# The second MLP matrix by Strassen's seven products, with split weights cached in DRAM

## Chip, cores, metric

One core of a Trainium2 chip. The metric is the device time of the whole program in microseconds (us), from the first to the last instruction of the core; lower is better.

## The reference, cut

```python
# SEQ = 2048 and DEC_SEQ = 512 rows of D_MODEL = 1024; D_FF = 4096; one layer, f32
h = rms_norm(x, norm_mix_g)
x = x + pool_mixer(h, pool_w, pool_scale)      # four channel groups: mean over 2, 4, 8, 16
                                               # neighbouring rows minus the row, then 256x256
h = rms_norm(x, norm_mlp_g)
a = relu(einsum('bsd,df->bsf', h, w_up))       # first matrix, 1024 x 4096
x = x + einsum('bsf,fd->bsd', a * a, w_down)   # second matrix, 4096 x 1024
y = rms_norm(x, final_norm_g)
```

Both inputs (2048 and 512 rows) go through the same layer. The time is nearly all in the two matrices.

## The kernel before

The 2560 rows are five **groups** of 512 rows (GT). A group keeps its normalized, transposed rows `h2` in SBUF and runs over the 4096 hidden columns in 16 **chunks** of 256 (two tiles of 128, FT). All five groups read all weights again.

**Precision by splitting.** Each f32 operand is split in two parts, hi (rounded to the type fp32r) and lo (the rest), and a product is three matmuls: hi x hi, hi x lo, lo x hi. ACT makes hi (a copy that casts), DVE makes lo (a subtraction). This is done to each tile of `w_up` (`wu_raw` to `wu_hi`, `wu_lo`, 128 x 1024), to each chunk of `w_down` (`wd_raw` to `wd_hi`, `wd_lo`) and to the squared activations `a`.

**PE's order** is written out by hand: `up(n+1)`, the first matrix of the next chunk (2 tiles x 8 x 3 matmuls of 512 columns), then `down(n)`, the second matrix (8 outputs x 2 tiles x 3 matmuls), so that activation and splits of a chunk lie behind the other matmuls. `up` writes `up_ps` (2 banks of PSUM), `down` a ring of four banks, `ring_ps`. DVE evicts each bank and adds it to `acc` (`add_down`); PE waits for `ring_read` before it writes a bank again.

**The next group's mixer** is woven into the first eight chunks of a group: for each of four windows ACT normalizes a column block of the rows, PE transposes it (`turn_window`, `turn_halos`), POOL adds neighbours (`window_sums`, window w has w+1 additions of some 1024 elements), DVE and ACT split, PE multiplies (`pool_out`), DVE adds. At a group's end PE also transposes the next group's rows (`transpose`), ACT and DVE make `h2_hi` and `h2_lo` from them, and the finished group is normalized and stored. POOL also squares the activations for `a_lo` (`squares`).

**SP's queue** issues all DMAs, in an order written out by hand, each behind a wait for the buffer to come free: for every chunk two `wu` tiles of 512 KB into two raw buffers, and one 1 MB `wd` chunk. An engine works its queue strictly in order, so a wait holds up all that stands behind it.

**Start and end.** The first group's mixer is done with banded matrices on PE; the last group's final norm and stores follow the last matmul.

Of the kernel before, what the change touches and what calls it, by code (L numbers as in the profile page):

```python
# [6 lines left out]
P = 128  # L27
# [44 lines left out]
FIRST = 0  # L72

SUM_STEPS = [sum(v + 2 for v in range(w)) for w in range(WINDOWS + 1)]


def build(nc, x, halos, w_up, w_down, pool_w, pool_scale, g_mix, g_mlp, g_fin, ends, bands, ident_in,
          out):
# [3 lines left out]
    ds = bass.ds  # L82
# [4 lines left out]
    with ctx:  # L87
# [23 lines left out]
        wd_hi = sb("wd_hi", [P, FT, D], f32r)  # L111
        wd_lo = sb("wd_lo", [P, FT, D], f32r)
        wu_raw = sb("wu_raw", [P, FT, DT, P])
        wu_hi = sb("wu_hi", [P, FT, DT, P], f32r)
        wu_lo = sb("wu_lo", [P, FT, DT, P], f32r)
        wd_raw = sb("wd_raw", [P, FT, D])

        relu = sb("relu", [P, FT, GT])
        square = sb("square", [P, FT, GT])
        a_hi = sb("a_hi", [P, 2, FT, GT], f32r)  # L120
        a_lo = sb("a_lo", [P, 2, FT, GT], f32r)

        wd_last_hi = h2_hi[:, 0:FT * NH, :]
        wd_last_lo = h2_lo[:, 0:FT * NH, :]
        acc = sb("acc", [P, TT, D])
# [5 lines left out]
        sums = [sb(f"sums{i}", [P, CT, HT]) for i in range(2)]  # L131
        end_scale = sb("end_scale", [P, WINDOWS, CT, 2, HALO])
        dt_hi = sb("dt_hi", [P, CT, GT], f32r)
        dt_lo = sb("dt_lo", [P, CT, GT], f32r)
        junk = dt_hi[:, :, :].rearrange("p c t -> p (c t)")
        x1 = sb("x1", [P, TT, D])
        pw_hi = sb("pw_hi", [P, WINDOWS * CT, WC], f32r)
        pw_lo = sb("pw_lo", [P, WINDOWS * CT, WC], f32r)
        g_fin_b = sb("g_fin_b", [P, D])
# [15 lines left out]
        ms_end = sb("ms_end", [P, 1])  # L155
        me_end = sb("me_end", [P, 1])
# [3 lines left out]
        pw_raw = acc[:, 0:2, :].rearrange("p a (b e) -> p (a b) e", e=WC)  # L160
        scale_b = acc[:, 2, :]


        row_squares = [x1[:, i, :] for i in range(TT)] + [junk]
        first_squares = square[:, :, :].rearrange("p c t -> p (c t)")

        wd_room = [wd_lo[:, t, :].rearrange("p (c t) -> p c t", c=CT) for t in range(FT)]
        first_dt = [(dt_hi[:, :, :], dt_lo[:, :, :]), wd_room,
                    (a_hi[:, 0, :, :], a_hi[:, 1, :, :]), (a_lo[:, 0, :, :], a_lo[:, 1, :, :])]
# [18 lines left out]
        acc_moved = sem("acc_moved")  # L188
# [19 lines left out]
        ring_read = sem("ring_read")  # L208
        xr_in = [sem(f"xr_in{j}") for j in range(TT)]
# [8 lines left out]
        pw_in = [sem(f"pw_in{w}") for w in range(WINDOWS)]  # L218
        banded = sem("banded")
# [28 lines left out]


        def ring_base(g):  # L250
            return FIRST_OUTS + g * GROUP_OUTS

        LAST_BASE = ring_base(GROUPS - 1)
        MIX_END = MIX_PAIRS * MIX_PAIR_OUTS

        def window_sums(engine, eng, w, ht, room, done_sem, done):

# [16 lines left out]

        @block.sync
        def _(sp):
            def load_wu(k, t):

                sp.dma_start(wu_raw[:, t, :, :], w_up[k, t]).then_inc(wu_in[t], 16)

            def next_wu(n, k):
                for t in range(FT):
                    sp.wait_ge(wu_lo_done, FT * (n - 1) + t + 1)
                    load_wu(k, t)

            def load_wd(k):
                sp.dma_start(wd_raw[:, :, :], w_down[k]).then_inc(wd_in, 16)

            def step(n, k, k_next):
                next_wu(n + 1, k_next)
                sp.wait_ge(wd_lo_done, FT * n)
                load_wd(k)
# [4 lines left out]

            def load_halos(m):  # L300
                sp.dma_start(xh[:, :], halos[m]).then_inc(halo_in, 16)

            def load_ends(m):
                sp.dma_start(end_scale[:, :, :, :, :], ends[m]).then_inc(ends_in, 16)

            def store(g):
                for j in range(TT if g is not LAST else TT - 1):
                    sp.wait_ge(final_done, TT * g + j + 1)
                    sp.dma_start(out[g, j * P:(j + 1) * P, :], acc[:, j, :]).then_inc(acc_moved, 16)
                if g is LAST:  # L310

                    j = TT - 1
                    for h in range(NH):
                        c = slice(h * HALF, (h + 1) * HALF)
                        sp.wait_ge(final_done, TT * g + j + 1 + h)
                        sp.dma_start(out[g, j * P:(j + 1) * P, c], acc[:, j, c]).then_inc(acc_moved, 16)

            def prefetch_rows(m):
                sp.wait_ge(transposed, DT * m)
                load_rows(m)  # L320
                sp.wait_ge(xw_done, NORMS * WINDOWS * (m - 1))
                load_halos(m)
                sp.wait_ge(summed, SUM_STEPS[WINDOWS] * (m - 1))
                load_ends(m)
# [9 lines left out]
            sp.dma_start(scale_b, pool_scale.partition_broadcast(P)).then_inc(acc_moved, 16)  # L334
# [5 lines left out]
            sp.dma_start(g_fin_b[:, :], g_fin.partition_broadcast(P)).then_inc(gain_in, 16)  # L340
            for t in range(FT):
                load_wu(0, t)
            load_wd(0)
            load_ends(1)
            load_halos(1)
            next_wu(1, 1)
            sp.wait_ge(transposed, DT)
            load_rows(1)
            next_wu(2, 2)

            def group(g, mixer, prefetch):
                n0 = CHUNKS * g
                sp.wait_ge(wd_lo_done, 2 * (n0 + 1))
                load_wd(1)
                with sp.Fori(2, CHUNKS - 1) as k:
                    step(n0 + k, k, k + 1)
                if mixer:
# [5 lines left out]
                if prefetch:  # L363
                    prefetch_rows(g + 2)
                if mixer:
                    next_wu(n0 + CHUNKS + 2, 2)
# [811 lines left out]
```

## Time and profile before

| | |
|---|---|
| runs | 1880.66, 1882.22, 1882.68 us; median 1882.22 |
| profiled execution | span 1879.7 us; the profile gives no other time of its own, so the span stands for it; the median of the runs is 2.5 us above |
| PE, DVE, ACT, POOL busy | 99%, 59%, 37%, 18% |
| granted TensorE clock | 0.997 of 2.4 GHz on average |
| DMA | 194.84 MB, 104 GB/s over the span, queue q1 29.7% of the 16 engines' time |

A page's group row reads: line, engine, operation, written tile <- read tiles, shape, count | busy us, mean ns of one | idle time of the engine just before, and who ended it. Matmuls overlap, so the mean of one (390 ns) is longer than the distance between two.

### The profile page before, as it was taken

What the parts mean: (1) busy time and instruction counts of PE and PEld (TensorE: products, weight loads), DVE (VectorE), ACT (ScalarE), POOL (GpSimd) and SP (SyncE); (2) the same over time, 40 slices, a digit from 0 to 9 for tenths busy, and PEclk for the clock granted to TensorE, in tenths of its full rate; (3) what the DMA queues carried; (4) which work ended last, traced back from release to release, by engine and by line L of the source; (5) the groups of instructions that cost most, each with busy time, mean ns of one, the idle gap of its engine ahead of it and who ended that gap; (6) DMA issues with size and microseconds to landing.
All of it is one profiled execution on the core that took longest, in us unless ns stands there. A gap on an engine that the chain in (4) does not pass through costs nothing.

```text
span 1879.7 us, 24832 instructions
## 1 busy us (share of the span) xinstructions
PE 1858.7 (99%) x8598; PEld 1548.4 (82%) x8598; DVE 1108.7 (59%) x1323; ACT 702.0 (37%) x1012; POOL 330.8 (18%) x300
## 2 busy tenths in 40 slices
PE   8999999999999999999999999999999999999998
PEld 7888888888888888888888888888888888888887
DVE  5566655566666555666665556566745575555555
ACT  5533342245333422453334224433352342233232
POOL 3222310012223100112231011222310110001011
PEclk9999999999999999999999999999999999999999
DMA  6422222243222222422222324322232232223221
GB/s 212 159 88 89 80 100 100 90 146 127 90 89 89 90 89 89 170 102 90 89 89 89 101 100 160 110 84 84 82 110 99 91 135 101 89 89 104 99 88 67
DMA packets 43975, 194.84 MB, mean 104 GB/s; under 512 B 5132, under 2 KB 7052, under 8 KB 33684
## 3 DMA queue, kind: packets, MB, share of 16 engines
q1 hardware_dynamic: 43924, 194.34, 29.7%
q14 instruction: 41, 0.34, 0.1%
q8 instruction: 10, 0.16, 0.0%
HBM read 183.84 MB, written 10.49 MB: 103 GB/s over the span
## 4 chain that ended last, share of the span: by engine, by line
PE 94%; DVE 3%; issue 2%; ACT 1%; DMA 0%; POOL 0%; SPq 0%; DVEq 0%; ACTq 0%; POOLq 0%
PE ring_ps L937 15%; PE ring_ps L939 15%; PE ring_ps L938 15%; PE up_ps L918 14%; PE up_ps L916 14%; PE up_ps L917 14%; DVE a_lo L621 1%; PE ring_ps L976 1%; PE ring_ps L978 1%; PE ring_ps L977 1%; PE mix_ps L997 1%; DVE wd_lo L615 1%; PE mix_ps L959 1%; DMA first_x<-x 0%; ACT wd_hi L389 0%
## 5 line engine op out<-in xcount | busy, mean ns | idle before, releaser
L629 DVE TENSOR_TENSOR acc<-ring_ps,acc 128x512 f32<-128x512 f32 x600 | 412.6, 690 | 420.6 <-PE ring_ps L939 419.3
L937 PE MATMUL ring_ps<-wd_hi,a_hi 128*128 128x512 f32 x1264 | 496.8, 393 | 5.2 <-DVE a_lo L621 2.7
L916 PE MATMUL up_ps<-h_hi,wu_hi 128*128 128x512 f32 x1280 | 499.9, 391 | 0.0
L917 PE MATMUL up_ps<-h_lo,wu_hi 128*128 128x512 f32 x1280 | 498.3, 389 | 0.0
L918 PE MATMUL up_ps<-h_hi,wu_lo 128*128 128x512 f32 x1280 | 498.2, 389 | 0.0
L939 PE MATMUL ring_ps<-wd_hi,a_lo 128*128 128x512 f32 x1264 | 492.5, 390 | 0.0
L938 PE MATMUL ring_ps<-wd_lo,a_hi 128*128 128x512 f32 x1264 | 492.0, 389 | 0.0
L821 POOL TENSOR_TENSOR square<-relu 128x512 f32<-128x512 f32 x160 | 176.5, 1104 | 1241.2 <-ACT relu L396 1198.3
L609 DVE TENSOR_TENSOR wu_lo<-wu_raw,wu_hi 128x1024 fp32r<-128x1024 f32 x158 | 202.6, 1282 | 219.0 <-ACT wu_hi L383 219.0
L389 ACT CAST wd_hi<-wd_raw 128x1024 fp32r<-128x1024 f32 x158 | 158.2, 1051 | 413.9 <-PE ring_ps L939 296.7
L937 PEld LDWEIGHTS ring_ps<-wd_hi,a_hi 128*128 128x128 f32 x1264 | 237.4, 188 | 56.8 <-DVE acc L629 5.0
L396 ACT ACTIVATE relu<-up_ps 128x512 f32<-128x512 f32 x160 | 95.6, 598 | 500.0 <-PE up_ps L918 500.0
L918 PEld LDWEIGHTS up_ps<-h_hi,wu_lo 128*128 128x128 f32 x1280 | 240.3, 188 | 50.0
L917 PEld LDWEIGHTS up_ps<-h_lo,wu_hi 128*128 128x128 f32 x1280 | 240.4, 188 | 49.0
L916 PEld LDWEIGHTS up_ps<-h_hi,wu_hi 128*128 128x128 f32 x1280 | 240.4, 188 | 48.9 <-DVE h_lo L654 0.2
L939 PEld LDWEIGHTS ring_ps<-wd_hi,a_lo 128*128 128x128 f32 x1264 | 237.2, 188 | 49.5
L938 PEld LDWEIGHTS ring_ps<-wd_lo,a_hi 128*128 128x128 f32 x1264 | 237.5, 188 | 47.8
L615 DVE TENSOR_TENSOR wd_lo<-wd_raw,wd_hi 128x1024 fp32r<-128x1024 f32 x158 | 220.9, 1439 | 51.6 <-ACT wd_hi L389 51.6
L383 ACT CAST wu_hi<-wu_raw 128x1024 fp32r<-128x1024 f32 x160 | 165.8, 1036 | 0.0
L621 DVE TENSOR_TENSOR a_lo<-square,a_hi 128x512 fp32r<-128x512 f32 x160 | 125.9, 827 | 0.0
L398 ACT ACTIVATE a_hi<-relu 128x512 fp32r<-128x512 f32 x160 | 101.2, 633 | 5.1
L267 POOL TENSOR_TENSOR sums<-sums 128x1024 f32<-128x1024 f32 (+3 forms) x24 | 66.4, 2766 | 1.9
(134 smaller groups left out, 854.2 us busy)
## 6 DMA issues: line engine op xcount, KB each, us to landing
wu_raw<-w_up SPq DMA_DIRECT2D x160, 512.0 KB, 3.3
wd_raw<-w_down SPq DMA_DIRECT2D x80, 1024.0 KB, 4.8
xr<-x SPq DMA_DIRECT2D x20, 512.0 KB, 7.0
out<-acc SPq DMA_DIRECT2D x19, 512.0 KB, 2.9
first_x<-x SPq DMA_DIRECT2D x4, 512.0 KB, 8.6
acc<-pool_w SPq DMA_DIRECT2D x4, 256.0 KB, 10.4
acc<-pool_scale SPq DMA_DIRECT2D x1, 512.0 KB, 10.3
g_fin_b<-g_fin SPq DMA_DIRECT2D x1, 512.0 KB, 10.7
```

The costliest lines, as they stand in the source:

```text
L383: nc.scalar.copy(wu_hi[:, t, :, :], wu_raw[:, t, :, :]).then_inc(wu_hi_done, 1)
L389: nc.scalar.copy(wd_hi[:, t, :], wd_raw[:, t, :]).then_inc(wd_hi_done, 1)
L609: nc.vector.tensor_tensor(wu_lo[:, t, :, :], wu_raw[:, t, :, :], wu_hi[:, t, :, :].bitcast(f32), ALU.subtract).then_inc(wu_lo_done, 1)
L615: nc.vector.tensor_tensor(wd_lo[:, t, :], wd_raw[:, t, :], wd_hi[:, t, :].bitcast(f32), ALU.subtract).then_inc(wd_lo_done, 1)
L629: nc.vector.tensor_tensor(acc[:, j, c], ring_ps[:, o % RING, :], base[:, j, c], ALU.add).then_inc(ring_read, 1)
L821: nc.gpsimd.tensor_tensor(square[:, t, :], relu[:, t, :], relu[:, t, :], ALU.mult).then_inc(square_done, 1)
L916: nc.tensor.matmul(o, wu_hi[:, t, d, :], h2_hi[:, d, :], start=(d == 0), stop=False)
L917: nc.tensor.matmul(o, wu_hi[:, t, d, :], h2_lo[:, d, :], start=False, stop=False)
L918: last = nc.tensor.matmul(o, wu_lo[:, t, d, :], h2_hi[:, d, :], start=False, stop=(d == DT - 1))
L937: nc.tensor.matmul(dst, a_hi[:, slot, t, r], hi, start=(t == 0), stop=False)
L938: nc.tensor.matmul(dst, a_hi[:, slot, t, r], lo, start=False, stop=False)
L939: last = nc.tensor.matmul(dst, a_lo[:, slot, t, r], hi, start=False, stop=(t == FT - 1))
```

## The change

The second matrix is computed by Strassen's algorithm in Winograd's form. A **step** n is 512 hidden columns of a group (8 steps a group, STEPS = 40). It has four tiles u = 4n to 4n+3 of the first matrix. Its share of the second matrix, activations (512 rows x 512 hidden) times weights (512 hidden x 1024, taken as two column halves), is cut into 2 x 2 quadrants, and seven products of quadrant sums take the place of eight. Product q = 7n+k writes two banks at once; the order is P5, P6, P1, P3, P4, P7, P2. Each product is summed over the 8 steps of a group in one of seven f32 accumulators (`m_acc`), and the seven are combined once per group (`combine_first`, `combine_rest`), after which `finish` scales the rows.

- PE: per step 12 matmuls a product, 84 instead of 96; the first matrix, the mixer and all column counts are unchanged. The products run one step behind the tiles: `step(n)` interleaves tiles 4n to 4n+3 with products q0 to q0+6, q0 = 7(n-1).
- DVE: sums of activation quadrants (`sum_a`, four of 512 elements a step) and, in group 0 only, of weight quadrants (`sum_w`, four of 1024); seven a splits of 512; seven evictions of 1024 (before: sixteen of 512).
- Weights of the second matrix: in group 0 the raw quadrants are loaded (two 1 MB loads a step), summed, split into one of three `w_slot`s, used, and stored to a DRAM cache (56 stores of 1 MB). In groups 1 to 4 SP loads the split operands back from the cache, seven 1 MB loads a step; `wd` is no more split there.
- `wu_raw` has one buffer instead of two.
- The square is now ACT's (`activate` squares in place), POOL has no squares. hi of a is an ACT copy.
- The pooling weights' split is cached in DRAM too and loaded for each window. The windows are woven into steps 3 to 6 of a group, its statistics into steps 2 and 7.
- Everything is unrolled; there are no loops in the program.

Core of the diff (in the order of the file; the parts left out are of the same pattern):

```diff
+P5, P6, P1, P3, P4, P7, P2 = range(7)
+NP = 7
+A_SLOTS = 2
+W_SLOTS = 3
+CACHED = PAIRS * NP
...
+            def load_wu(u):
+                if u > 0:
+                    sp.wait_ge(wu_lo_done, u)
+                s, f = u // FP % PAIRS, u % FP
+                sp.dma_start(wu_raw[:, :, :], w_up[2 * s + f // FT, f % FT]).then_inc(wu_in, 16)
+            def load_raw(n, k):
+                if n > 0:
+                    sp.wait_ge(w_lo_done, NP * (n - 1) + (P7 if k == 0 else P2) + 1)
+                sp.dma_start(wd_raw[:, 2 * k:2 * k + 2, :], w_down[2 * n + k]).then_inc(raw_in[k], 16)
+            def move_w(q):
+                if q < CACHED:
+                    sp.wait_ge(w_lo_done, q + 1)
+                    sp.dma_start(w_cache[q], slot).then_inc(w_stored[i], 16)
+                elif q < PRODUCTS:
+                    sp.wait_ge(ring_full, TURN[q - W_SLOTS] + 1)
+                    if q - W_SLOTS < CACHED:
+                        sp.wait_ge(w_stored[i], 16 * stores_of_slot(q))
+                    sp.dma_start(slot, w_cache[q % CACHED]).then_inc(w_in[i], 16)
...
+            def step(n):
+                q0 = NP * (n - 1)
+                if n > 0:
+                    move_w(q0 + 3)
+                load_wu(4 * n + 3)
+                if n > 0:
+                    move_w(q0 + 4)
+                    move_w(q0 + 5)
+                if 0 < n < PAIRS:
+                    load_raw(n, 0)
+                load_wu(4 * n + 4)
+                if n > 0:
+                    move_w(q0 + 6)
+                if 0 < n < PAIRS:
+                    load_raw(n, 1)
+                move_w(q0 + 7)
+                load_wu(4 * n + 5)
+                move_w(q0 + 8)
+                move_w(q0 + 9)
+                load_wu(4 * n + 6)
+            for n in range(STEPS + 1):
+                step(n)
+                if is_boundary(n):
+                    store(n // PAIRS - 1)
...
+            def split_wu(u):
+                act.wait_ge(wu_in, 16 * (u + 1))
+                if u >= FT:
+                    act.wait_ge(up_done, u - FT + 1)
+                nc.scalar.copy(wu_hi[:, u % FT, :, :], wu_raw[:, :, :]).then_inc(wu_hi_done, 1)
...
+            def boundary(n):
+                for k in range(3):
+                    split_h2(g, 2 * k)
+                    split_h2(g, 2 * k + 1)
+                    split_a(q0 + 2 + k)
+                    split_w(q0 + 3 + k)
+                split_h2(g, DT - 2)
+                split_h2(g, DT - 1)
+                split_a(q0 + 5)
+                split_w(q0 + 6)
+                activate(4 * n)
+                split_wu(4 * n + 2)
+                split_a(q0 + 6)
+                activate(4 * n + 1)
+                split_wu(4 * n + 3)
+                final_stats(g - 1)
...
+            def step(n):
+                split_wu(4 * n + 2)
+                if n > 0:
+                    evict(q0 + 0)
+                    split_a(q0 + 2)
+                    evict(q0 + 1)
+                    split_w(q0 + 3)
+                    split_a(q0 + 3)
+                    sum_a(n - 1, P7)
+                    split_w(q0 + 4)
+                split_wu(4 * n + 3)
+                if n > 0:
+                    evict(q0 + 2)
+                    split_a(q0 + 4)
+                    split_w(q0 + 5)
+                    evict(q0 + 3)
+                    split_a(q0 + 5)
+                    split_w(q0 + 6)
+                if windows:
+                    subtract_own(g + 1, w)
+                    split_pooled(g + 1, w)
+                split_wu(4 * n + 4)
+                if n > 0:
+                    evict(q0 + 4)
+                    split_a(q0 + 6)
+                sum_w(n, P5)
+                sum_w(n, P7)
+                split_w(q0 + 7)
+                sum_w(n, P6)
+                if n > 0:
+                    evict(q0 + 5)
+                split_w(q0 + 8)
+                sum_w(n, P4)
+                if windows:
+                    add_pooled(g + 1, w)
+                split_wu(4 * n + 5)
+                sum_a(n, P5)
+                split_a(q0 + 7)
+                sum_a(n, P6)
+                if n > 0:
+                    evict(q0 + 6)
+                split_a(q0 + 8)
+                sum_a(n, P3)
+                split_w(q0 + 9)
...
+            def product(q):
+                r, a, b = TURN[q], q % A_SLOTS, q % W_SLOTS
+                pe.wait_ge(a_lo_done, q + 1)
+                if q < CACHED:
+                    pe.wait_ge(w_lo_done, q + 1)
+                else:
+                    pe.wait_ge(w_in[b], 16 * loads_of_slot(q))
+                if r >= 2:
+                    pe.wait_ge(ring_read, r - 1)
...
+            def step(n):
+                up_tile(4 * n)
+                if windows:
+                    turn_window(g + 1, w)
+                product(q0 + 0)
+                product(q0 + 1)
+                if windows:
+                    turn_halos(g + 1, w)
+                up_tile(4 * n + 1)
+                product(q0 + 2)
+                product(q0 + 3)
+                up_tile(4 * n + 2)
+                product(q0 + 4)
+                product(q0 + 5)
+                if windows:
+                    pool_out(g + 1, w)
+                up_tile(4 * n + 3)
+                product(q0 + 6)
+            def boundary(n):
+                pe.wait_ge(x1n_done, TT * g)
+                for k in range(4):
+                    transpose(g, 2 * k)
+                    transpose(g, 2 * k + 1)
+                    product(q0 + k)
+                pe.wait_ge(h2_lo_done, DT * (g + 1))
+                up_tile(4 * n)
+                product(q0 + 4)
+                product(q0 + 5)
+                up_tile(4 * n + 1)
+                product(q0 + 6)
+                up_tile(4 * n + 2)
+                up_tile(4 * n + 3)
```

`boundary(n)` stands in place of `step(n)` at n = 8, 16, 24, 32, the first step of a group. DVE's boundary has, between the split pairs of `h2`, one eviction, a split (and w split in group 0's last products) each; then `combine_first` (five additions of 1024), `split_wu(4n+2)`, evictions 4 and 5 with split 6, `combine_rest` (two), `split_wu(4n+3)`, eviction 6, `split_wu(4n+4)`, `finish`, `split_wu(4n+5)` and the first sums and splits of step n.

## Rows read from the trace of the kernel before

**Rows 1.** The page's busy times: engine, us, share of the span, instructions.

```profile
PE 1858.7 (99%) x8598; PEld 1548.4 (82%) x8598; DVE 1108.7 (59%) x1323; ACT 702.0 (37%) x1012; POOL 330.8 (18%) x300
```

**Rows 2.** Waits of PE, the longest of its MLP's: us in total, times, longest.

```profile
PE ring_ps L937 <- DVE a_lo L621: 2.7, 4, 0.7
```

**Rows 3.** Timeline of PE: first, two middle and last 512-column matmul; start, length.

```profile
42.67 0.50 PE L916 MATMUL up_ps<-h_hi,wu_hi 128*128 128x512 f32 x1
...
499.77 0.39 PE L918 MATMUL up_ps<-h_hi,wu_lo 128*128 128x512 f32 x1
...
516.99 0.39 PE L937 MATMUL ring_ps<-wd_hi,a_hi 128*128 128x512 f32 x1
...
1872.76 0.39 PE L939 MATMUL ring_ps<-h_hi,a_lo 128*128 128x512 f32 x1
```

**Rows 4.** Timeline of PE: the first and last of 20 pooling matmuls; eight transposes.

```profile
28.39 0.28 PE L976 MATMUL ring_ps<-pw_hi,wd_lo 128*128 128x256 f32 x1
...
30.64 0.28 PE L977 MATMUL ring_ps<-pw_lo,wd_lo 128*128 128x256 f32 x1
...
387.76 1.03 PE L997 MATMUL mix_ps<-ident,xr 128*128 128x128 f32 x8
```

**Rows 5.** Timeline of DVE, splits with nothing on POOL.

```profile
57.48 1.23 DVE L609 TENSOR_TENSOR wu_lo<-wu_raw,wu_hi 128x1024 fp32r<-128x1024 f32 x1 [4.14 <-ACT wu_hi L383]
58.62 2.35 DVE L615 TENSOR_TENSOR wd_lo<-wd_raw,wd_hi 128x1024 fp32r<-128x1024 f32 x2
60.90 1.29 DVE L621 TENSOR_TENSOR a_lo<-square,a_hi 128x512 fp32r<-128x512 f32 x2
```

**Rows 6.** The page's groups: an eviction, and ACT's two sizes.

```profile
L629 DVE TENSOR_TENSOR acc<-ring_ps,acc 128x512 f32<-128x512 f32 x600 | 412.6, 690 | 420.6 <-PE ring_ps L939 419.3
...
L383 ACT CAST wu_hi<-wu_raw 128x1024 fp32r<-128x1024 f32 x160 | 165.8, 1036 | 0.0
...
L398 ACT ACTIVATE a_hi<-relu 128x512 fp32r<-128x512 f32 x160 | 101.2, 633 | 5.1
```

**Rows 7.** The page's DMA issues: KB each, median us from issue to landing.

```profile
wu_raw<-w_up SPq DMA_DIRECT2D x160, 512.0 KB, 3.3
wd_raw<-w_down SPq DMA_DIRECT2D x80, 1024.0 KB, 4.8
...
out<-acc SPq DMA_DIRECT2D x19, 512.0 KB, 2.9
```

**Rows 8.** Timeline of SP's queue at a group boundary: start, length, issue.

```profile
406.04 0.33 SPq L289 DMA_DIRECT2D wd_raw<-w_down  x1
406.64 2.09 SPq L298 DMA_DIRECT2D xr<-x  x4
...
411.51 0.34 SPq L281 DMA_DIRECT2D wu_raw<-w_up  x1
```

**Rows 9.** Line L298 (xr), its last three issues of 406.64 to 408.73.

```profile
DMA to landing us min/median/max: 6.7/7.4/8.5
```

**Rows 10.** DMA issues: the wu load of 411.51 alone.

```profile
wu_raw<-w_up SPq DMA_DIRECT2D x1, 512.0 KB, 6.9
```

**Rows 11.** Timeline of DVE and POOL in window 3: work side by side.

```profile
223.13 8.46 POOL L267 TENSOR_TENSOR sums<-sums 128x1048 f32<-128x1048 f32 x3
...
222.01 4.99 DVE L615 TENSOR_TENSOR wd_lo<-wd_raw,wd_hi 128x1024 fp32r<-128x1024 f32 x2 [0.70 <-ACT wd_hi L389]
```

**Rows 12.** Windows of the start: busy of PE PEld DVE ACT POOL, PEclk, DMA.

```profile
9.00:12.00 3.00, 0.34 (x4) 0.16 (x2) 0.34 (x1) 1.15 (x2) 0.75 (x2) 1.00 1.03 249
12.00:15.00 3.00, 2.83 (x14) 2.83 (x15) 1.66 (x4) 1.15 (x2) 1.23 (x2) 0.56 1.04 380
```

**Rows 13.** Timelines of the end: ACT, DVE, SP; start, length.

```profile
1873.91 0.63 ACT L408 ACTIVATE dt_hi<-acc 128x512 fp32r<-128x512 f32 x1 [0.20 <-DVE acc L629]
...
1873.18 0.69 DVE L629 TENSOR_TENSOR acc<-ring_ps,acc 128x512 f32<-128x512 f32 x1 [0.24 <-PE ring_ps L939]
...
1876.56 0.99 SPq L316 DMA_DIRECT2D out<-acc  x2
```

More of the change, by code:

```diff
@@ L278, in _ @@
         def _(sp):
[L279 to L294, printed above, removed]
+            def load_wu(u):
+                if u >= UPS:
+                    return
+                if u > 0:
[7 more added lines that the diff above has]
+            def move_w(q):
+                i = q % W_SLOTS
+                slot = w_slot[:, i, :, :, :].rearrange("p s k e -> p (s k e)").bitcast(f32)
+                if q < CACHED:
[6 more added lines that the diff above has]
+                    sp.dma_start(slot, w_cache[q % CACHED]).then_inc(w_in[i], 16)
             def load_rows(m):
@@ L339, in _ @@
             sp.dma_start(g_mlp_c[:, :], g_mlp).then_inc(gain_in, 16)
[L340 to L357, printed above, removed]
-                    step(n0 + CHUNKS - 1, CHUNKS - 1, 0)
-                    step(n0 + CHUNKS, 0, 1)
-                else:
-                    sp.wait_ge(wd_lo_done, 2 * (n0 + CHUNKS - 1))
-                    load_wd(CHUNKS - 1)
[L363 to L366, printed above, removed]
-                store(g)
@@ L376, in _ @@
+            for n in range(STEPS + 1):
+                step(n)
+                if is_boundary(n):
+                    store(n // PAIRS - 1)
+            sp.wait_ge(out_moved, 16 * TT * GROUPS)
         @block.scalar
         def _(act):
-            def split_wu(n, t, first=False):
-                act.wait_ge(wu_in[t], 16 * (n + 1))
-                if not first:
-                    act.wait_ge(up_done, FT * (n - 1) + t + 1)
-                nc.scalar.copy(wu_hi[:, t, :, :], wu_raw[:, t, :, :]).then_inc(wu_hi_done, 1)
@@ L605, in _ @@
+            for n in range(STEPS):
+                if is_boundary(n):
+                    boundary(n)
+                else:
+                    step(n)
+            for k in range(2, NP):
+                split_a(NP * (STEPS - 1) + k)
+            final_stats(LAST)
         @block.vector
         def _(dve):
-            def split_wu(n, t):
-                dve.wait_ge(wu_hi_done, FT * n + t + 1)
-                nc.vector.tensor_tensor(wu_lo[:, t, :, :], wu_raw[:, t, :, :], wu_hi[:, t, :, :].bitcast(f32),
-                                        ALU.subtract).then_inc(wu_lo_done, 1)
@@ new lines, in _ @@
+            for n in range(STEPS):
+                if is_boundary(n):
+                    boundary(n)
+                else:
+                    step(n)
+            q0 = NP * (STEPS - 1)
+            evict(q0 + 0)
+            split_a(q0 + 2)
+            evict(q0 + 1)
+            split_a(q0 + 3)
+            sum_a(STEPS - 1, P7)
+            evict(q0 + 2)
+            split_a(q0 + 4)
+            evict(q0 + 3)
+            split_a(q0 + 5)
+            combine_first(LAST)
+            evict(q0 + 4)
@@ L813, in _ @@
+            split_a(q0 + 6)
+            evict(q0 + 5)
+            combine_rest(LAST)
+            evict(q0 + 6)
+            finish(LAST)
         @block.gpsimd
         def _(pool):
-            def squares(n, first=False):
-                for t in range(FT):
-                    pool.wait_ge(relu_done, FT * n + t + 1)
-                    if not first:
-                        pool.wait_ge(a_lo_done, FT * (n - 1) + t + 1)
-                    nc.gpsimd.tensor_tensor(square[:, t, :], relu[:, t, :], relu[:, t, :],
-                                            ALU.mult).then_inc(square_done, 1)
@@ L1024, in _ @@
                 pe.wait_ge(pool_lo, w + 1)
+                part = slice(w * CT, (w + 1) * CT)
                 for j in range(TT):
@@ L1091, in _ @@
[L1091 to L1103 removed]
+            for f in range(FP):
+                up_tile(f, next_tile if f == 0 else lambda d: None)
@@ L1106, in end_scales @@
+            for n in range(1, STEPS):
+                if is_boundary(n):
+                    boundary(n)
+                else:
+                    step(n)
+            for k in range(NP):
+                product(NP * (STEPS - 1) + k)
 def end_scales():
```

886 lines of the change are left out of this document (474 added, 412 removed).

## Prediction

> **What bounds the kernel now.** I read the page's busy times first: PE is busy for 99% of the span, DVE for 59%, ACT and POOL less [rows 1]. Then the waits: those of the MLP's matmuls are small: the greatest, for `a_lo`, sums to 2.7 us [rows 2]. Then the timeline of PE: the 512-column matmuls follow each other every (516.99-499.77)/76 = 0.2267 us [rows 3], at the full granted clock. So the kernel is TensorE work laid end to end, from the first matmul of the first matrix at 42.67 to the last end at 1873.15, 1830.5 us [rows 3]. The work in it: 7680 matmuls x 0.2267 = 1741.1; 384 of the pooling at 0.118 = 45.5 and about 300 transposes at 0.11 = 33 [rows 4]; some 1820 in all, so PE's own stalls there are about 10.7 us. 42.7 us lie before and 6.6 behind.
>
> **What the change takes away.** Each step of 512 hidden columns costs 84 instead of 96 matmuls for the second matrix, over 40 steps: 480 x 0.2267 = -108.8 us. This is sure as far as PE sets the time. A step is now four tiles of the first matrix at 24 x 0.2267 = 5.44 and seven products at 12 x 0.2267 = 2.72: 40.8 us.
>
> **What must keep up, and its prices.** DVE: a 1024-element subtraction costs 1.22 us alone and 1.14 in a row, 512 elements 0.61 in a row [rows 5]; an eviction of 512 from PSUM is 0.69 [rows 6], so one of 1024 is an estimated 1.14 (0.69 plus another 512 elements, less the overlap). ACT: 1.04 and 0.63 [rows 6]. Handing over to another engine: 0.07 (taken a little above the 0.04 between the end of DVE's last eviction, 1873.87, and ACT's start on it, 1873.91, [rows 13]). DMA: 512 KB land after 3.3 us and 1 MB after 4.8 [rows 7], so 1.8 fixed and 1.5 per 512 KB. Transfers that are issued together queue: behind a 1 MB load issued at 406.04 (by the median landed at 410.9), four of 512 KB landed until 408.4+8.5 = 416.9 (the last was issued at 408.4), 1.5 us each, and a wu load issued at 411.5 behind them took 6.9 instead of 3.3 [rows 8 to 10].
>
> **Groups 1 to 4, ordinary steps: nothing.** DVE per step: four wu splits, seven evictions, seven a splits, four a sums: 4x1.14 + 7x1.14 + 11x0.61 = 19.3 of 40.8. The weights now come by DMA: 7 MB of slots and 2 MB of wu per step, 9x3.0 = 27 of 40.8 us. I walked the SP queue: each slot's load is issued at the end of the product three before; the shortest lead is 10.9 us against 4.8 to 7.8. The single-buffered wu_raw is refilled after its split and has 5 us to spare. So PE sets these steps.
>
> **Group 0: a ring through SP's queue, +139.** Here each product's weights are summed and split on the chip and stored: 7 w splits and 4 w sums more, DVE 19.3+12.5 = 31.9 of 40.8. Throughput is enough; latency isn't. SP's queue alternates `move_w(q)` (waits for the w split of q, then a 1 MB store) and `load_wu(u)`, and DVE's queue puts the split of tile u between the w splits. So each wu load sits behind the store just issued: 1.8+3x1.5 = 6.3 us (1 MB and 512 KB). Walk one round from the end of w split 5 (offset of the product in q0; T=0):
> - store 5, raw load 0 and wu load 4n+4 are queued: 0.1+1.8+5x1.5 = 9.4; ACT hi and DVE lo 2.4: 11.8. Evict 4, a 6, sum P5 are 2.9; sum P7 waits for raw load 1, which ends 9x1.5 of traffic, at 15.4; it and w split 7: 17.8.
> - store 7, wu load 4n+5: 6.4, hi and lo 2.4: 26.5. a sum, a split 7 (hi, lo in turn 1.4), sum, evict 6, a 8, sum, w 9: 6.2: 32.7.
> - store 9, wu load 4n+6 and its splits 8.7: 41.4. Evict 0, a 2, evict 1, w 3: 4.1: 45.5.
> - store 3, wu load 4n+7 and its splits 8.8: 54.3. Evict 2, a 4, w 5: 2.9: 57.2.
>
> The round closes at 57.2 us and PE isn't in it; PE waits at products 6, 0, 2 and 4. In the four steps with a pooling window the third tile also waits for `pool_out`, whose second half needs the eviction of product 5 (late in DVE's queue, at 20): +4.0, and POOL's additions double the time of DVE's SBUF work beside them (two 1024-element splits 4.99 us instead of 2.35, [rows 5, 11]): +1.5. What is queued behind DVE's wu split are evictions and a splits, and PE's next product waits for these.
>
> Start: tiles 0 to 3 run undisturbed to 66.1. From the split of tile 4 at 64.9 sum P5, sum P7 and w split 0 end at 68.3; store 0 and wu load 5 bring that split to 77.1; sums, a splits 0 and 1 and w split 2 follow, to 82.9; store 2 and wu load 6, splits and evictions: w split 3 at 95.7; store 3, wu load 7 and the rest: w split 5 of step 1 at 107.4. Six rounds and four windows: 107.4+6x57.2+4x5.5 = 472.6; 32.7 more, and the boundary of step 8, walked likewise (transposed tiles' splits now in DVE's queue between evictions), ends at 551. Pure PE work would be there at 42.7+36x5.44+56x2.72+15.8 (windows)+5.1 (transposes, first tile) = 411.8. The term is +139. The store behind which a load queues is not in this trace: I take it to cost what a load ahead costs (a store alone takes 2.9 against a load's 3.3 [rows 7], so it moves its bytes about as fast). The bound below is that stores delay no load.
>
> The Trainium skill says the same, in "DMA: Bandwidth & Descriptors", section "Queues, rings and completion order": a completion increment lands only after every earlier write of that DMA engine. The rows show it for loads, none shows it for a store ahead. By it the term stays +139; by independent stores it would be the 58 of the second rival.
>
> **Boundaries 16, 24 and 32: +25.3 each, +76.** PE's order is transposes and products 0 to 3, tile 4n, products 4, 5, tile 4n+1, product 6. SP's is load of slot 3, `load_wu(4n+3)`, slots 4, 5, `load_wu(4n+4)`, slot 6. `load_wu(4n+3)` waits for the split of tile 4n+2, which ACT starts when tile 4n is done: activation 1.2, hi 1.1, lo 1.2 (DVE is still at `combine_first`, 5x1.14), then SP, then 512 KB and 1 MB: 1.8+4.5. So product 4 waits 10.1 us behind tile 4n; product 6 waits for `load_wu(4n+4)` in the same way, 9.9. Ahead of these, product 0 has no tile before it to cover the last sum and split of a (1.9), and the transposes wait for bank reads that stand in DVE's queue between evictions and splits (2.5): 4.4. Product 0 of the next step waits 0.9 for `finish`. The bounds: if SP had slots 4 to 6 issued before the wu loads, 5.4 each; if they queued behind more traffic than these, a few us more.
>
> **Clock: +8.** PE was busy for 0.34 of the three microseconds to 12.0, and in the next three the granted clock was 0.56 (mostly the lower of 1.2 and 2.4 GHz), which loses 0.44x3 = 1.3 [rows 12]. Six pauses of 10 us at the boundaries: 8. In group 0 PE isn't on the path and a slower matmul is hidden.
>
> **End: +8.** In the last seven products `combine_first` stands in DVE before eviction 4 and split 6: 9.3 us from the end of product 3 to product 6 instead of 5.4, and 0.8 at product 0: +4.7. Behind the last matmul, where DVE's last eviction now ends 0.7 us after it: an eviction that ends 1.9 after it, two squares of full rows one after the other (2x1.25, by ACT's 0.63 for half a row and its read-out), then the same root, scale and store as now; 9.9 instead of 6.6: +3.3. The prices are those of the last rows' chain [rows 13].
>
> **Sum**, against the profiled execution's 1879.7: -108.8 -10.7 +139 +76 +8 +8 = 1991; the runs' median is 2.5 above that span: 1994, said as 1995.
>
> **Rivals.**
> - *Faster: the loads are in time.* If the wu load is never what DVE waits for, a step of group 0 is PE-bound (31.9 of DVE in 40.8), and the slots of a boundary arrive before tile 4n ends. Boundaries then cost 5.4 each, 4x5.4 = 22: 1879.7+2.5-108.8-10.7+8+22 = 1793. It decides if a load is on hand about 4 us after w split in all four places; for it speaks that DMA is only 30% busy now (the table above) and that a wu load alone lands in 3.3; against it SP's order, since `load_wu` can't be issued before the store ahead of it, and the lead left by 40.8 us is less than the walk's parts.
> - *Stores don't delay loads.* Only loads queue behind loads. The four parts of the round are then 14.4, 12.4, 10.2 and 9.1: 46.1 us. Seven rounds save 78 and the start 3, so group 0 costs 58 instead of 139; the boundaries, where only loads queue, stay: 1994-81 = 1913.
> - *More in group 0*: halved clock at PE's pauses there reaches the path in the window steps, small stalls in the windows of groups 1 to 3, and a round of 60: 7x2.8 + 4x3 + 8 = 40 more: 2035.
>
> **How the numbers follow.** Forecast 0.56, stores independent 0.16, loads in time 0.14, more in group 0 0.14. The forecast's own range is 1950 to 2020. I take 1885 to 2045, which leaves out the loads in time and part of the last. Within 0.2% (3.8 us, what a measurement of this kernel can tell from no change) and below come only from the first rival and the gap between it and the second: faster 0.14, same 0.02, slower 0.84.
>
> **What would show it.** 3360 matmuls of the second matrix at 0.2267 apart; in group 0 a period of about 57 us with DVE's wu split waiting for ACT, ACT for wu_raw's DMA; PE busy only some 72% there and 99% in ordinary steps later; two pauses of 10 us at each of three boundaries, ended by the slot's DMA, with a lower clock behind them. I am wrong if the period in group 0 is near 41, or if the slots' loads at a boundary land before tile 4n ends.

## The result, and the profile after

The changed kernel takes 2006.7 us (median of four runs, 2003.3 to 2010.8) where the kernel before takes 1881.4 on the same chip: ratio 1.0666, interval 1.0649 to 1.0683. It is 6.7% slower with 480 fewer matmuls. The forecast was 1995, and slower. The profiled execution has a span of 2007.2 us.

The page of the changed kernel: busy times, granted clock in 40 slices, the chain by engine, two groups and the DMA issues.

```profile
PE 1809.7 (90%) x8118; PEld 1493.7 (74%) x8118; DVE 1136.6 (57%) x1178; ACT 762.8 (38%) x1186; POOL 147.1 (7%) x139
...
PE   8878778777999999977999999699999977999996
...
PEclk8998799889999999988999999799999988999998
...
PE 69%; DVE 12%; DMA 9%; issue 5%; ACT 3%; SPq 1%; POOL 0%; POOLq 0%; ACTq 0%; DVEq 0%
...
L706 DVE TENSOR_TENSOR wu_lo<-wu_raw,wu_hi 128x1024 fp32r<-128x1024 f32 x158 | 201.7, 1276 | 660.2 <-ACT wu_hi L460 660.1
...
L460 ACT CAST wu_hi<-wu_raw 128x1024 fp32r<-128x1024 f32 x160 | 165.9, 1037 | 129.2 <-DMA wu_raw<-w_up 128.9
...
w_slot<-w_cache SPq DMA_DIRECT2D x224, 1024.0 KB, 5.6
wu_raw<-w_up SPq DMA_DIRECT2D x160, 512.0 KB, 5.4
w_cache<-w_slot SPq DMA_DIRECT2D x56, 1024.0 KB, 4.9
wd_raw<-w_down SPq DMA_DIRECT2D x16, 1024.0 KB, 8.7
```

Read it in this order. TensorE has lost 480 matmuls and 49 us of busy time, but its share fell from 99% [rows 1] to 90%. The slices say where: the first ten (group 0), and a 7 or 6 in slices 18 and 19, 26, 33 and 34, which are the boundaries at steps 16, 24 and 32; the last slice holds the end. In between it is full. ScalarE's split of the first matrix's weights waited for no DMA before [rows 6]; now it waits 129 us. The median landing of that load went from 3.3 [rows 7] to 5.4 us.

Group 0, the timeline of VectorE in step 2 to 3 of the changed kernel, the splits of `w_slot` (L715) and of `wu` (L706) that bound the four parts of the forecast's round (the bracket is VectorE's idle time just before, and who ended it):

```profile
165.12 1.22 DVE L715 TENSOR_TENSOR w_slot<-wd_raw,w_slot 128x1024 fp32r<-128x1024 f32 x1
...
177.37 1.23 DVE L706 TENSOR_TENSOR wu_lo<-wu_raw,wu_hi 128x1024 fp32r<-128x1024 f32 x1 [8.16 <-ACT wu_hi L460]
...
191.19 1.22 DVE L706 TENSOR_TENSOR wu_lo<-wu_raw,wu_hi 128x1024 fp32r<-128x1024 f32 x1 [2.40 <-ACT wu_hi L460]
...
205.90 1.22 DVE L706 TENSOR_TENSOR wu_lo<-wu_raw,wu_hi 128x1024 fp32r<-128x1024 f32 x1 [7.19 <-ACT wu_hi L460]
...
218.34 1.23 DVE L706 TENSOR_TENSOR wu_lo<-wu_raw,wu_hi 128x1024 fp32r<-128x1024 f32 x1 [3.05 <-ACT wu_hi L460]
...
221.21 1.22 DVE L715 TENSOR_TENSOR w_slot<-wd_raw,w_slot 128x1024 fp32r<-128x1024 f32 x1
```

The same stretch on SyncE's queue:

```profile
183.95 0.33 SPq L352 DMA_DIRECT2D w_cache<-w_slot  x1
184.32 0.43 SPq L338 DMA_DIRECT2D wu_raw<-w_up  x1
187.55 11.51 SPq L352 DMA_DIRECT2D w_cache<-w_slot  x2
199.11 0.43 SPq L338 DMA_DIRECT2D wu_raw<-w_up  x1
```

And on ScalarE the split that the load of 184.32 releases:

```profile
190.11 1.05 ACT L460 CAST wu_hi<-wu_raw 128x1024 fp32r<-128x1024 f32 x1 [0.69 <-DMA wu_raw<-w_up]
```

W split 5 recurs after 221.21-165.12 = 56.1 us (58.3 a round earlier; forecast 57.2), and a wu split closes each part with a wait for ScalarE. The load of 184.32 stands 0.37 behind a 1 MB store and is released 5.8 us later, where such a load alone took 3.3 [rows 7] and the forecast had 6.3.

The boundary at step 16, SyncE's queue:

```profile
887.50 0.33 SPq L338 DMA_DIRECT2D wu_raw<-w_up  x1
887.88 0.91 SPq L357 DMA_DIRECT2D w_slot<-w_cache  x2
909.94 0.33 SPq L338 DMA_DIRECT2D wu_raw<-w_up  x1
910.31 0.91 SPq L357 DMA_DIRECT2D w_slot<-w_cache  x2
```

And the first matmuls of products 4 and 6 on TensorE:

```profile
893.49 0.77 PE L1119 MATMUL ring_ps<-w_slot,a_slot 128*128 128x512 f32 x1 [9.51 <-issue]
...
916.11 0.77 PE L1119 MATMUL ring_ps<-w_slot,a_slot 128*128 128x512 f32 x1 [9.69 <-issue]
```

The slot loads go out only behind the wu load, and the product starts when the first of them has landed (issued at 887.88, landed at 893.40 by the trace, product 4 at 893.49). The profile writes these waits down to "issue", since no releaser was recorded; the queue's rows give the reason, and the experiment e2 below shows it.

Windows of the changed kernel: 250 us of group 0, 180 us inside group 1, and the end of the first pause (busy of PE, PEld, DVE, ACT, POOL, then the granted clock, DMA share, GB/s).

```profile
180.00:430.00 250.00, 193.01 (x820) 158.80 (x820) 164.22 (x150) 95.80 (x141) 29.47 (x14) 0.88 0.53 192
640.00:820.00 180.00, 180.00 (x858) 150.84 (x857) 108.44 (x105) 66.45 (x107) 23.79 (x14) 1.00 0.57 219
...
888.00:892.00 4.00, 0.00 (x0) 0.00 (x0) 0.00 (x0) 0.00 (x0) 0.00 (x0) 0.50 0.90 330
892.00:894.00 2.00, 0.51 (x1) 0.50 (x2) 0.00 (x0) 0.00 (x0) 0.00 (x0) 0.50 1.04 434
894.00:897.00 3.00, 3.00 (x8) 2.31 (x7) 0.00 (x0) 0.00 (x0) 0.00 (x0) 0.50 0.36 150
897.00:900.00 3.00, 3.00 (x14) 2.47 (x13) 1.71 (x2) 0.62 (x1) 0.00 (x0) 0.95 0.00 0
```

In group 0 TensorE is busy for 77% of the time at a clock of 0.88 (forecast some 72%), in group 1 for all of it. Each product that ends one of these pauses starts at half clock.

### The profile page after: what moved, and what is told of

Its sections match the earlier page's. It is cut to its first block, busy times and chain, and to the rows that moved or that the text cites. A ratio compares the mean times of both kernels' runs of the same rounds, so it can differ in the third digit from the quotient of the medians.

```text
span 2007.2 us, 20672 instructions
## 1 busy us (share of the span) xinstructions
PE 1809.7 (90%) x8118; PEld 1493.7 (74%) x8118; DVE 1136.6 (57%) x1178; ACT 762.8 (38%) x1186; POOL 147.1 (7%) x139
## 4 chain that ended last, share of the span: by engine, by line
PE 69%; DVE 12%; DMA 9%; issue 5%; ACT 3%; SPq 1%; POOL 0%; POOLq 0%; ACTq 0%; DVEq 0%
PE up_ps L1100 11%; PE up_ps L1102 11%; PE up_ps L1101 11%; PE ring_ps L1119 10%; PE ring_ps L1120 10%; PE ring_ps L1121 10%; DMA wu_raw<-w_up 9%; DVE m_acc L783 2%; DVE w_slot L715 2%; ACT wu_hi L460 2%; DVE a_slot L724 2%; DVE wu_lo L706 2%; PE ring_ps L1144 1%; PE ring_ps L1146 1%; PE ring_ps L1145 1%
## 5 line engine op out<-in xcount | busy, mean ns | idle before, releaser
L706 DVE TENSOR_TENSOR wu_lo<-wu_raw,wu_hi 128x1024 fp32r<-128x1024 f32 x158 | 201.7, 1276 | 660.2 <-ACT wu_hi L460 660.1
L1119 PE MATMUL ring_ps<-w_slot,a_slot 128*128 128x512 f32 x1120 | 455.2, 406 | 115.6 <-issue 58.2
L1120 PE MATMUL ring_ps<-w_slot,a_slot 128*128 128x512 f32 x1120 | 448.1, 400 | 0.0
L1121 PE MATMUL ring_ps<-w_slot,a_slot 128*128 128x512 f32 x1120 | 447.0, 399 | 0.0
L783 DVE TENSOR_TENSOR m_acc<-ring_ps,m_acc 128x1024 f32<-128x1024 f32 x245 | 298.8, 1220 | 106.5 <-PE ring_ps L1121 106.1
L1119 PEld LDWEIGHTS ring_ps<-w_slot,a_slot 128*128 128x128 f32 x1120 | 217.6, 194 | 172.2 <-DVE a_slot L724 67.0
L496 ACT ACTIVATE a_raw<-up_ps 128x512 f32<-128x512 f32 x160 | 95.3, 596 | 558.0 <-PE up_ps L1102 557.7
L1121 PEld LDWEIGHTS ring_ps<-w_slot,a_slot 128*128 128x128 f32 x1120 | 217.5, 194 | 47.3
L1120 PEld LDWEIGHTS ring_ps<-w_slot,a_slot 128*128 128x128 f32 x1120 | 218.0, 195 | 44.1
L460 ACT CAST wu_hi<-wu_raw 128x1024 fp32r<-128x1024 f32 x160 | 165.9, 1037 | 129.2 <-DMA wu_raw<-w_up 128.9
L488 ACT CAST a_slot<-s_sum 128x512 fp32r<-128x512 f32 x160 | 99.3, 621 | 269.8 <-PE ring_ps L1121 135.1
L724 DVE TENSOR_TENSOR a_slot<-s_sum,a_slot 128x512 fp32r<-128x512 f32 x160 | 135.1, 844 | 30.9 <-ACT a_slot L488 30.9
L488 ACT CAST a_slot<-a_raw 128x512 fp32r<-128x512 f32 x120 | 74.5, 621 | 99.7 <-PE ring_ps L1121 99.7
L498 ACT ACTIVATE a_raw<-a_raw 128x512 f32<-128x512 f32 x160 | 101.1, 632 | 5.1
L724 DVE TENSOR_TENSOR a_slot<-a_raw,a_slot 128x512 fp32r<-128x512 f32 x120 | 81.8, 681 | 0.0
L321 POOL TENSOR_TENSOR sums<-ht 128x1024 f32<-128x1024 f32 (+3 forms) x16 | 34.5, 2159 | 639.7 <-ACT ht L532 639.7
```

The source lines that it names most:

```text
L460: nc.scalar.copy(wu_hi[:, u % FT, :, :], wu_raw[:, :, :]).then_inc(wu_hi_done, 1)
L488: nc.scalar.copy(a_slot[:, q % A_SLOTS, 0, :, :], a_source(q)).then_inc(a_hi_done, 1)
L498: nc.scalar.activation(a, a, ACT.Square).then_inc(sq_done, 1)
L706: nc.vector.tensor_tensor(wu_lo[:, u % FT, :, :], wu_raw[:, :, :], wu_hi[:, u % FT, :, :].bitcast(f32), ALU.subtract).then_inc(wu_lo_done, 1)
L724: nc.vector.tensor_tensor(a_slot[:, i, 1, :, :], a_source(q), a_slot[:, i, 0, :, :].bitcast(f32), ALU.subtract).then_inc(a_lo_done, 1)
L783: nc.vector.tensor_tensor(dst, src, dst, ALU.add).then_inc(ring_read, 1)
```

## The experiments

The kernel before was timed beside them on the same chips: 1880.9 and 1882.5 us in the first two sets, 1882.4 in the last. "Product 0 of step 9" is the time at which TensorE starts it in the profiled execution: 561.5 in the changed kernel. Up to there lies group 0, with the boundary of step 8. e1, e2, e4 and e6 were run once each, the others four to six times.

**e1_wu_first.** In steps 0 to 7 each load of the first matrix goes ahead of the store it stood behind; no instruction is added or removed.

```diff
+                if n < PAIRS:
+                    load_wu(4 * n + 3)
+                    if n > 0:
+                        move_w(q0 + 3)
+                        move_w(q0 + 4)
+                    load_wu(4 * n + 4)
+                    if n > 0:
+                        move_w(q0 + 5)
+                        load_raw(n, 0)
...
```

> SP issues each wu load of steps 0 to 7 ahead of the store before which it stood behind (the load needs only the previous wu split), nothing else is changed. The forecast's theory (a ring through SP's queue: w split, store, wu load behind it, wu split, w split): the wu loads land about 3.3 to 5 us after the previous wu split, the ring is gone, a plain step of group 0 takes 41 to 45 us instead of 57, and the whole 85 to 110 us less than the changed kernel, about 1910. First rival, DVE's amount of work bounds group 0 (32 to 38 us busy of a step plus its hand-overs): less than 20 us gained. Second rival, the halved clock in PE's pauses makes group 0 slow: some 20 us gained at most, since the pauses at windows stay.

Measured: 1943.3 us; span 1941.5, against 2007.2: -65.7. Nearly all of it lies in group 0 (product 0 of step 9 at 497.4, 64.1 earlier). From product 0 of one step to that of the next it now takes 43.7 us in step 1 and 43.5 in step 7 (57.8 and 54.5 in the changed kernel): there the ring is gone, as expected. In step 2 it is 51.0 (56.5), and in the window steps 3 to 6 it is 55.0 to 58.7 (62.0 to 67.2): there something else takes over. On the page, the wait of ScalarE's split for its load (129.2 us in the changed kernel) is nearly gone:

```profile
L479 ACT CAST wu_hi<-wu_raw 128x1024 fp32r<-128x1024 f32 x160 | 165.6, 1035 | 17.2 <-DMA wu_raw<-w_up 16.6
```

The order of the queue is a cause, but gives back 64 us where 85 to 110 were expected.

**e2_slots_first.** At steps 16, 24 and 32 SyncE issues the loads of slots 3 to 6 ahead of the wu loads.

```diff
+                if is_boundary(n) and n > PAIRS:
+                    for k in range(3, 7):
+                        move_w(q0 + k)
+                    load_wu(4 * n + 3)
+                    load_wu(4 * n + 4)
...
```

> At the boundaries 16, 24 and 32 SP issues the loads of slots 3 to 6 ahead of the two wu loads, nothing else is changed. Theory of the forecast: the two pauses of 9.5 us at products 4 and 6 go (3 x 19.3 = 58) and with them the half clock behind each (6 x 1.9 = 11): 69 us less, about 1938. Rival, DVE's combining and splitting there would make PE wait anyway for activations or evictions: at most half of that.

Measured: 1935.3 us (span 1933.5), -71.5 from the changed kernel by the medians. Group 0 is as it was (product 0 of step 9 at 561.4). From there to product 0 of step 17 it takes 351.3 us instead of 376.9, and no wait of TensorE there is over 1.93 us. The 10 us pauses are the wu loads' wait in SyncE's queue.

**e4_store_twice.** Every store of the weight cache is issued a second time, to a tensor that nothing reads. A slot is also reused only after both of its stores, but ScalarE, which splits into the slots, shows no wait for a store in the trace. Its wait for the wu loads up to product 0 of step 9 went from 122.5 to 182.6 us.

```diff
                     sp.dma_start(w_cache[q], slot).then_inc(w_stored[i], 16)
+                    sp.dma_start(w_copy[q], slot).then_inc(w_stored[i], 16)
```

> Each of the 56 stores of a w slot is issued twice (the second to another DRAM tensor, and a slot is reused only after both), the order is that of the changed kernel. Theory that a load queues behind the stores ahead of it: each of the four wu loads of a round lands 3.0 us later (1 MB more), a round takes 69 instead of 57 and the whole 84 + about 9 in the first step and boundary more: about 2100. Rival, stores don't delay loads: no change, 2007 +- 5. Between the two if the stores use the queue only in part.

Measured: 2087.3 us, +80.6. Product 0 of step 9 comes at 638.9, 77.4 later, so the loss is again in group 0. Four places in a round, 7.5 rounds: 77.4/30 = 2.6 us for each 1 MB store ahead of a load, near the 3.0 that the forecast took (in the two rounds ahead of the windows, 70.9 and 68.8 instead of 58.3 and 56.1, it is 3.2). The page's DMA issues show the second store behind the first, and `wd_raw`'s load behind both at 11.0 instead of 8.7:

```profile
w_cache<-w_slot SPq DMA_DIRECT2D x56, 1024.0 KB, 3.9
w_copy<-w_slot SPq DMA_DIRECT2D x56, 1024.0 KB, 7.1
wd_raw<-w_down SPq DMA_DIRECT2D x16, 1024.0 KB, 11.0
```

This excludes the rival in which stores delay no load. The rule of the Trainium skill that the prediction names ("DMA: Bandwidth & Descriptors", "Queues, rings and completion order") agrees with it, for stores ahead of loads as for loads. Whether the load is held by that order or by the time that both transfers need on the same DMA engines, no run here separates.

**e3_both.** The edits of e1 and e2 together.

> Both orders together. Theory: the two gains add, since they lie in different groups: about 2007 - 100 - 69 = 1838, which is below the kernel before (1881). Rivals: if group 0 is bound by DVE, about 1920.

Measured: 1872.2 us, ratio to the kernel before 0.9952 (0.9936 to 0.9967): half a per cent faster, but 34 us above what was expected. That is e1's shortfall: product 0 of step 9 comes at 498.0, and from there to that of step 17 it takes 352.8, as in e2. A part of what was missed shows on TensorE ahead of a pooled window of group 0:

```profile
208.48 0.58 PE L1174 MATMUL ring_ps<-pw_slot,dt_hi 128*128 128x256 f32 x1 [8.25 <-DVE m_acc L813]
```

On VectorE the eviction of product 5 (L813 at 207.22) stands behind a sum, one that waits for the raw load, a split, and a third sum:

```profile
198.92 1.22 DVE L766 TENSOR_TENSOR t_sum<-wd_raw 128x1024 f32<-128x1024 f32 x1
203.68 1.23 DVE L770 TENSOR_TENSOR wd_raw<-wd_raw 128x1024 f32<-128x1024 f32 x1 [3.54 <-DMA wd_raw<-w_down]
204.82 1.22 DVE L745 TENSOR_TENSOR w_slot<-t_sum,w_slot 128x1024 fp32r<-128x1024 f32 x1
206.07 1.23 DVE L774 TENSOR_TENSOR t_sum<-wd_raw,t_sum 128x1024 f32<-128x1024 f32 x1
207.22 1.22 DVE L813 TENSOR_TENSOR m_acc<-ring_ps,m_acc 128x1024 f32<-128x1024 f32 x1
```

**e5_evict_early.** e3, and in the window steps that eviction goes ahead of the weight sums.

```diff
                     split_a(q0 + 6)
+                    if windows:
+                        evict(q0 + 5)
                 sum_w(n, P5)
                 sum_w(n, P7)
                 split_w(q0 + 7)
                 sum_w(n, P6)
-                if n > 0:
+                if n > 0 and not windows:
                     evict(q0 + 5)
```

> The changed kernel with both new orders of SyncE's queue (e3_both) and one more move: in the window steps VectorE empties the pair of banks of product 5 right behind the split of activation quadrant 6, ahead of the weight sums of P5 and P7, instead of behind the sum of P6. In e3_both TensorE waits 7 to 11 us ahead of the pooled window in each of the four window steps of group 0, because that eviction stands behind two or three sums and splits of VectorE. If the order of VectorE sets this wait, it falls to about 2 us, some 20 to 25 us in all: about 1850. Rival: VectorE is simply full there (the same work stands on it, in another order), or the ring through ScalarE and the raw loads sets the step: the wait moves to the next products, no more than 5 us: 1867 to 1875.

Measured: 1853.3 us, 0.9852 (0.9835 to 0.9868). 19 us from one instruction's place in four steps. At the same window TensorE doesn't wait; 4.3 us remain at product 6 behind it, for VectorE's additions of the window (L849):

```profile
212.51 0.76 PE L1151 MATMUL ring_ps<-w_slot,a_slot 128*128 128x512 f32 x1 [4.34 <-DVE xr L849]
```

**e6_no_group0_work.** A bound: group 0 loads its operands ready made, seven a step as in groups 1 to 4. Raw loads, sums and splits of weights and the stores of the cache are left out, and the slot loads go first at all four boundaries. The operands are other data of the same size, so the values computed are not those of the reference.

> A bound, with part of the computation left out: the changed kernel in which group 0 takes its split weight operands ready made, by loads like groups 1 to 4 (of the split pooling weights in DRAM, so the numbers are not those of the reference): no raw load, no weight sum, no split on ScalarE or VectorE, no store of the cache; SyncE issues the four operand loads first at all boundaries. Theory: all that group 0 costs beyond the pure matmuls is this work and its stores, and the 30 us of each boundary are the order of the queue: about 1800. Rival: a part of the loss lies in the products' own chain (sums and splits of the activations, evictions, the ring of banks), which stays here: then 1820 to 1840.

Measured: 1800.5 us in one run (span 1798.7, product 0 of step 9 at 426.7). TensorE is busy for 98% of the span. So the work of group 0 still costs e5 53 us, and the products' own chain of sums, splits and evictions costs little: product 0 of step 9 stands 10 us behind the 417 that TensorE's work alone gives in the forecast's walk.

**e7_sums_on_pool.** e5, with the sums P5 and P7 made by GpSimd, at the end of each of its steps but ahead of the means of the mixed rows.

```diff
+                if n < PAIRS:
+                    pool.wait_ge(raw_in[0], 16 * (n + 1))
+                    if n > 0:
+                        pool.wait_ge(w_lo_done, NP * (n - 1) + P4 + 1)
+                    nc.gpsimd.tensor_tensor(t, b_quad(0, 1), b_quad(0, 0), ALU.subtract).then_inc(t_done, 1)
...
```

> e5_evict_early, and of each step of group 0 the first two of the four weight sums (P5 and P7) are made by GpSimd, which has next to nothing to do there, instead of VectorE. VectorE loses two tensor operations of 1024 columns in each of eight steps, about 2.35 us each, so 4.7 us of the round of each step. If VectorE's share of the round sets it, 8 x 3 to 4.7 = 25 to 38 us less than e5: 1815 to 1830. Rival: GpSimd takes 4 to 5 us for such an operation and slows VectorE beside it (as its passes over the pooled window did), and the sum comes later than from VectorE: no change from e5, or some 5 us more.

Measured: 1860.9 us, 7.6 more than e5. The rival's number, but not its reason. TensorE starts the last matmul of step 7's last tile at 405.3, 4.4 ahead of e5, but then waits 13.4 us ahead of product 6 (its activations stand behind the rows below in ScalarE's queue). GpSimd's queue holds up the normalisation of the next group: the means of the mixed rows stand behind two sums that wait for the raw loads. Its timeline in e7:

```profile
406.01 2.34 POOL L1125 TENSOR_TENSOR wd_raw<-wd_raw 128x1024 f32<-128x1024 f32 x1 [3.90 <-DMA wd_raw<-w_down]
408.30 0.20 POOL L1055 TENSOR_TENSOR me_m<-ms_m,eps 128x4 f32<-128x4 f32 x1
408.58 1.02 POOL L1057 TENSOR_TENSOR rs_m<-me_m,power 128x4 f32<-128x4 f32 x1
```

And ScalarE's:

```profile
409.64 3.23 ACT L578 ACTIVATE x1n<-xr,rs_m 128x1024 f32<-128x1024 f32 x3 [18.59 <-POOL rs_m L1057]
```

**e8_statistics_first.** e7 with those two blocks exchanged.

```diff
+                if g < LAST and s == MIXED_STEP:
+                    mixed_rms(g + 1)
                 if n < PAIRS:
...
-                if g < LAST and s == MIXED_STEP:
-                    mixed_rms(g + 1)
```

> e7_sums_on_pool with two blocks of GpSimd's order exchanged in step 7: the means of the mixed rows (rs_m, on which ScalarE's normalisation of the next group waits) are made ahead of the two weight sums, which wait for the raw loads of W_down. In e7 TensorE ended step 7 4.4 us ahead of e5 (405.3 against 409.6), but ScalarE then waited 18.6 us for rs_m, TensorE 13.8 us ahead of product 0, and product 0 of step 9 came 8.4 us later than in e5 (485.1 against 476.8). If this wait behind GpSimd's sums is the whole loss of e7, the 4.4 us come through: 1849, and 1847 to 1851. Rival: the sums on GpSimd are too slow at the boundary as well: 1853 to 1861.

Measured: 1850.0 us, 0.9828 (0.9810 to 0.9847). It takes back the whole loss of e7 and 3.3 us more. (The wait in e7 that the expectation puts ahead of product 0 stands ahead of product 6 of step 7.) Its 1850.0 is the lowest median found, though its interval and that of e5 overlap.

## Why the prediction was right, step by step

The profiled execution took 2007.2 against a sum of 1991: 16 us short.

- **Matmuls, -108.8: right.** 8598-8118 = 480 are gone, and ordinary and window steps of groups 1 to 3 run without a pause (TensorE busy for 180.00 of 180 us). e6, with the same products, has a span 28 us above the 1770.9 that this term alone gives: 10 up to product 0 of step 9, 17 at the three later boundaries, 12 at the end, less the 10.7 of stalls that the kernel before had and the forecast took off. So that term is borne out too.
- **Group 0, +139: right in mechanism, 5 short.** Anchors of the walk: w split 5 of step 1 ends at 108.0 (forecast 107.4), the next two rounds take 58.3 and 56.1 (57.2), the four with a window 63.9, 62.5, 64.2 and 62.4 (62.7). Product 0 of step 9 starts at 561.5, where the walk has it at 556.3. The queue is on the path: swapping loads and stores alone gives back 64 us (e1), and doubling the stores costs 77 more (e4). The order is not the whole term, though: see below.
- **Stores delay loads as loads do: right.** This was taken without a row. By e4 a store costs 2.6 us ahead of a load, against 3.0 by the sizes.
- **Boundaries, +76: right, 3 less. Clock, +8: less than half of the 17.6 that came.** From product 0 of step 9 to that of step 33 the periods are 376.9, 375.4 and 375.8 us, where TensorE's work is 32x5.44+56x2.72+15.8 (windows)+3.5 (transposes) = 345.7: 30 each with the clock, against 28. The two pauses, 9.9 and 10.1 with the matmul's own 0.2, are as forecast (10.1 and 9.9). The clock cost more: behind the six pauses it stays at half for 3.5 to 5.2 us, where matmuls follow each other every 0.427 us instead of 0.227, which costs 1.7 to 2.5 us each and 12.6 in all. Another 1.6 to 1.7 come three times where none was forecast, at product 0 of step 9 and behind a wait of only 1.93 us at product 0 of the boundaries 24 and 32. That makes 17.6 us; without it the three periods are 73 above TensorE's work, against 76. The second pause, and the short wait at step 24:

```profile
917.00:921.00 4.00, 4.00 (x11) 3.03 (x11) 0.00 (x0) 0.00 (x0) 0.00 (x0) 0.50 0.14 57
921.00:923.00 2.00, 2.00 (x10) 1.67 (x9) 1.23 (x1) 0.13 (x1) 0.00 (x0) 0.95 0.00 0
...
1238.00:1242.00 4.00, 3.47 (x8) 2.75 (x9) 3.93 (x6) 1.78 (x3) 0.00 (x0) 0.58 0.77 317
```

- **End, +8: 4 short.** Behind the last matmul stand 12.8 us instead of 9.9, and the waits ahead of it are 0.9 more. ScalarE's squares of all four row tiles wait for `combine_rest` on VectorE, which ends as TensorE does, so four squares stand in a row behind the last matmul and not two:

```profile
1994.88 1.06 ACT L565 ACTIVATE dt_hi<-m_acc 128x1024 fp32r<-128x1024 f32 x1 [8.52 <-DVE m_acc L811]
...
1998.64 1.06 ACT L565 ACTIVATE dt_hi<-m_acc 128x1024 fp32r<-128x1024 f32 x1
```

- **The rivals.** "Stores don't delay loads" fell to e4. "The loads are in time" did not happen. It was priced at 1793; with both orders mended (e3) the kernel takes 1872, so that price was too low for the one other order that was tried: it took the weights' sums, raw loads and splits as hidden in 40.8 us, because VectorE's 31.9 fit. Only with them gone does the kernel come near it (e6, 1800). "More in group 0" named 40 us of stalls, and 5 came in group 0.

What the forecast did not see is a second layer under the first. With wu loads in time, 80 us of group 0's 144 stay (497.4 against 417, which is the forecast's 556.3 less its 139). e5 and e6 split them: some 21 are one eviction behind weight sums, 50 go with the rest of group 0's own work, about 10 stay without it. Of the 50, some may be the single-buffered `wd_raw`: in e3 VectorE waits 3.54 us for it above. In e5, from 60 to 480 us, TensorE's own waits are 20.3 us for splits of the activations, 12.1 for VectorE's additions of the window and 5.5 for evictions ahead of `pool_out`. How the 50 divide between raw loads and the engines' time was not tried.

## What to carry to other kernels

Caching operands in DRAM puts stores into a queue that also carries loads: order them by which one an engine waits for soonest, and check every boundary where a load's own wait blocks others behind it. Two moves of the issues, with no work changed, turned 6.7% slower into 0.5% faster. An engine that is half idle is no proof of cover; follow one round of its queue, look for the instruction behind a wait that another engine needs, and after each repair look again, since the next such instruction becomes the bound (e3 to e5, e7 to e8).

## What was not expected of the hardware

- The granted clock fell to 0.50 during a 9.5 us pause and stayed there for 3.8 us of full work behind it, and for 5.1 us behind the next, where the start-up rows [rows 12] had suggested a loss of 1.3 us. A pause of 10 us cost about 12.
- GpSimd takes 2.40 us for a subtraction of 1024 elements that VectorE makes in 1.22, and it holds up VectorE's work beside it. Splits of `a_slot` from `a_raw` (512 elements) have a mean of 0.97 us in group 0 of e7 and 0.68 in e5, but the mean hides two kinds: 20 of the 24 take 0.68 as before, and the four that start while a sum runs on GpSimd take 2.15 to 2.56 and end 0.55 us after the sum. An eviction from PSUM that starts at 195.99, beside a sum of 196.01, still takes 1.22. From e7, GpSimd, then VectorE:

```profile
298.70 2.37 POOL L1122 TENSOR_TENSOR t_sum<-wd_raw 128x1024 f32<-128x1024 f32 x1 [13.09 <-DMA wd_raw<-w_down]
...
297.93 1.22 DVE L813 TENSOR_TENSOR m_acc<-ring_ps,m_acc 128x1024 f32<-128x1024 f32 x1
299.06 2.56 DVE L754 TENSOR_TENSOR a_slot<-a_raw,a_slot 128x512 fp32r<-128x512 f32 x1
```

Moving two sums per step, 2.4 us of VectorE, gained 0.3 (e8) to 0.5 us (e7) per step up to the end of step 7's last tile; a split that is held up costs 1.5 to 1.9 of the 2.4.
